# A two-layer decoder step on one core: layer 1's sparse attention reordered around its index scores, the third expert's gate and up weights loaded during the router, a split first chunk and split final stores

## The reference, cut to what matters

```python
def _dsa_attention(q, k, v, qi, ki, wi, q_pos):
    n_sel = min(TOPK_MAX, nk // 4)                 # 64 of 256 keys (prompt), 256 of 1032 (sample)
    def one(blk):
        dots = jnp.einsum('bqhd,bkd->bqhk', bqi, ki)             # 8 index heads of 64
        score = jnp.einsum('bqh,bqhk->bqk', bwi * idx_scale, jax.nn.relu(dots))
        score = jnp.where(mask[None], score, -jnp.inf)
        _, idx = lax.top_k(score, n_sel)
        ...                                         # gather the selected keys and values
        s = jnp.einsum('bqhgd,bqkhd->bqhgk', bq, ks) * (HD_B ** -0.5)   # 16 heads on 4 key heads of 64
        p = jax.nn.softmax(jnp.where(valid, s, -jnp.inf), axis=-1)
        o = jnp.einsum('bqhgk,bqkhd->bqhgd', p, vs)

x = _layer_norm(ALPHA * x + h, ...)
x = _layer_norm(ALPHA * x + _moe(x, ...), ...)      # one of 4 groups, 2 experts in it; d_ff 512
x = x + sigmoid(x @ ple_gate_w[i] + ple_gate_b[i]) * (p[i] @ ple_proj[i])
```

## Time and profile before

| what | value |
| --- | --- |
| median of 3 runs | 1469.85 us (1469.12 to 1471.43) |
| profiled execution, its own time | 1466.78 us |
| its span | 1465.0 us |
| mean granted TensorE clock | 0.923 of full speed |
| PE busy | 1221.9 us, 83% of the span |
| DVE busy | 490.7 us, 33% |
| ACT busy | 343.6 us, 23% |
| POOL busy | 42.0 us, 3% |
| HBM read and written | 341.48 and 21.97 MB, 248 GB/s over the span |

### The profile page before, as it was taken

The page is one execution under the profiler, slowest core; times in us unless marked ns, Lnnn a source line. Parts: engine busy times, 40 slices in busy tenths (PEclk is TensorE's granted clock), DMA queues, the critical chain, the costliest instruction groups (busy, mean ns, idle before and its releaser), DMA issues.

```text
span 1465.0 us, 19098 instructions
## 1 busy us (share of the span) xinstructions
PE 1221.9 (83%) x6655; PEld 615.5 (42%) x6656; DVE 490.7 (33%) x1067; ACT 343.6 (23%) x807; POOL 42.0 (3%) x70
## 2 busy tenths in 40 slices
PE   6998888869589999995999831799884999999855
PEld 3445666645333333332444501556542333333322
DVE  1012555532611111116211679544242111111163
ACT  1113444441111112111111410455310212121110
POOL 1100000001000000001000100000100000000100
PEclk8999999999699999997999965999986999999978
DMA  9935799967248999995511433153440979999721
GB/s 336 414 135 209 266 351 373 344 265 317 87 189 349 363 425 426 423 421 172 211 37 30 137 120 110 44 187 116 151 152 12 390 287 408 424 426 424 299 85 36
DMA packets 97599, 364.50 MB, mean 249 GB/s; under 512 B 17856, under 2 KB 34272, under 8 KB 75760
## 3 DMA queue, kind: packets, MB, share of 16 engines
q1 hardware_dynamic: 88512, 328.79, 58.0%
q0 software_dynamic: 6320, 25.78, 5.1%
q10 hardware_dynamic: 2688, 8.91, 1.6%
HBM read 341.48 MB, written 21.97 MB: 248 GB/s over the span
## 4 chain that ended last, share of the span: by engine, by line
PE 72%; DVE 13%; DMA 6%; issue 4%; ACT 4%; POOL 0%; DVEq 0%; SPq 0%; POOLq 0%; ACTq 0%
PE PS L574 17%; PE PS L856 14%; PE PS L877 7%; PE PS L829 6%; PE PS L985 5%; DMA ring<-in_moe_w_up 3%; PE PS L707 2%; PE PS L670 2%; PE PS L657 2%; DVE PR L2043 2%; DVE PR L2041 2%; PE PS L838 2%; PE PS L608 1%; PE PS L1174 1%; PE PS L866 1%
## 5 line engine op out<-in xcount | busy, mean ns | idle before, releaser
L574 PE MATMUL PS<-ring,XT 128*128 128x512 f32 (+3 forms) x960 | 255.2, 478 | 12.5 <-DMA ring<-in_a_w_in 7.0
L856 PE MATMUL PS<-ring,QKV 128*64 128x512 f32 (+1 forms) x512 | 228.7, 595 | 6.8 <-ACT QKV L1206 3.9
L859 PE MATMUL PS<-ring,QKV 128*64 128x512 f32 (+1 forms) x512 | 228.5, 595 | 0.0
L1206 ACT ACTIVATE QKV<-PS 128x512 f32<-128x512 f32 (+5 forms) x180 | 95.0, 528 | 393.2 <-PE PS L574 156.6
L574 PEld LDWEIGHTS PS<-ring,XT 128*128 128x128 f32 (+1 forms) x960 | 121.0, 165 | 144.7 <-issue 127.2
L856 PEld LDWEIGHTS PS<-ring,QKV 128*64 128x64 f32 (+1 forms) x512 | 71.2, 141 | 151.5 <-issue 145.6
L877 PE MATMUL PS<-ring,QKV 128*64 128x512 f32 (+1 forms) x512 | 123.8, 598 | 0.0
L829 PE MATMUL PS<-X,QKV 128*64 128x512 f32 x432 | 103.3, 614 | 19.2 <-issue 19.2
L1850 DVE TENSOR_TENSOR QKV<-QKV,PS 64x512 f32<-64x512 f32 (+1 forms) x32 | 21.7, 680 | 234.3 <-ACT QKV L1390 234.3
L1855 DVE COPY QKV<-PS 64x512 f32<-64x512 f32 (+1 forms) x32 | 22.2, 693 | 189.1 <-PE PS L877 189.1
L985 PE MATMUL PS<-ring,XT 128*128 128x512 f32 (+1 forms) x256 | 74.8, 507 | 7.7 <-ACT XT L1206 7.7
(11 more groups left out here) (284 smaller groups left out, 1305.5 us busy)
## 6 DMA issues: line engine op xcount, KB each, us to landing
ring<-in_moe_w_gate SPq DMA_DIRECT2D x32, 2048.0 KB, 11.1
ring<-in_moe_w_up SPq DMA_DIRECT2D x32, 2048.0 KB, 15.8
ring<-in_moe_w_down SPq DMA_DIRECT2D x32, 2048.0 KB, 13.4
ring<-in_cache_a_k SPq DMA_DIRECT2D x64, 512.0 KB, 5.8
ring<-in_cache_a_v SPq DMA_DIRECT2D x64, 512.0 KB, 5.6
ring<-in_a_w_in SPq DMA_DIRECT2D x6, 2048.0 KB, 20.2
places<-OR POOLq DMA_DIRECT2D x8, 1024.0 KB, 19.1
ring<-in_ple_gate_w SPq DMA_DIRECT2D x4, 2048.0 KB, 13.4
```

Source lines behind the costliest of these rows:

```text
L574: ins = pe.matmul(PS[p0:p1, banks[u % 4], 0:c1 - c0], XT[:, k, t0:t0 + rows], wt[:, k, c0:c1], start=(k == 0), stop=(k == KD - 1))
L856: ins = pe.matmul(PS[0:m, 0, :], XE[:, k, 0:m], wg[:, k, :], start=(k == 0), stop=(k == KD - 1))
L859: ins = pe.matmul(PS[p1:p1 + m, 1, :], XE[:, k, 0:m], wu[:, k, :], start=(k == 0), stop=(k == KD - 1))
L1206: ins = act.activation(dst, src, ACT.Copy) if scale is None else \
```

## The change

The diff has 1365 lines. Its parts are:

1. **Start.** The first chunk of `a_w_in` comes as two loads of 1 MB with a semaphore each (`first_columns_landed` for the first), and PE waits for the second one only at its fifth matmul. POOL's load of the 955.5 KB of constants moves behind its small loads and waits for the first half chunk. Only the upper 64 rows of each expert's `places` are zeroed, by 16 DMAs in place of 8.
2. **Third expert.** The buffers QB, OR, KP, PR and SM become one tensor (WIDE), and expert 2's gate and up weights are loaded into it: the gate when the logits are there, the up weights when the norm is done. The first two pairs of experts are written out ahead of PE's loop, which starts at pair 2. SP then loads expert 4's gate and up as soon as expert 0's are used. POOL loads the second norm's parameters, which lie in the same buffer, after expert 2 has used its up weights.
3. **Layer 1.** The columns of `b_w_in` are loaded in another order, the index columns first, as two chunks of 292; the kidx pages come right after them, then the other three chunks, then all keys, then all values. PE turns the tokens and projects the index columns only (tiles 0, 2, 1), turns the kidx pages, computes prompt index scores (by 64-row halves of the operands, with no zeroes) and sample scores; only then come the nine other units, while DVE selects for the prompt and sorts for the sample. A half of the sort has 520 columns. q and k are rotated after the sort. All keys and queries are turned ahead of the batches, the keys in place in the ring. The selection runs on 128 partitions at once. In the batches, prompt scores use 64-row halves, the values of request b-1 are multiplied within batch b, and the prompt's values come out transposed, so that no turn of outputs follows.
4. **End.** Six stores, each as soon as its half of a tile is ready.

```diff
+B_COLUMNS = ((1536, 1828), (1828, 2120), (0, 512), (512, 1024), (1024, 1536))
+INDEX_UNITS = ((0, 0, 7), (1, 0, 5), (0, 2, 6), (1, 2, 4), (0, 1, 7), (1, 1, 5))
...
-            for j in range(5):
-                s.add(("b_in", j), ("qkv_mm1", 3 * j + 3))
-            s.add("kidx", ("kidx_mm", 8), DB * NPAGE)
+            for j in range(2):
+                s.add(("b_in", j), ("qkv_mm1", 5 + j))
+            s.add("kidx", ("sis_mm", 9), DB * NPAGE)
+            for j in range(2, 5):
+                s.add(("b_in", j), ("qkv_mm1", 3 * j + 3))
             for pr in range(4):
-                s.add(("kb", pr), ("kbt_mm", 8 * pr + 8), 2 * NPAGE)
+                s.add(("kb", pr), ("sb_mm", 2 * pr + 2), 2 * NPAGE)
+            for pr in range(4):
                 s.add(("vb", pr), ("pvb_mm", 2 * pr + 2), 2 * NPAGE)
...
-        HALF = 512 + NS
+        HALF = 512 + DQ
...
+            w0 = a_w_in[0].rearrange("(p k) n -> p k n", k=KD)
+            s0 = place(("a_in", 0))
+            for half, sem in ((0, S("first_columns_landed")), (1, landed[s0])):
+                sp.dma_start(ring[:, s0, 2048 * half:2048 * half + 2048].rearrange("p (k n) -> p k n", k=4),
+                             w0[:, 4 * half:4 * half + 4, 0:512]).then_inc(sem, 16)
...
+                sp.wait_ge(*at(f"logit_mm{layer}", 1))
+                load(2, 0, EARLY[0], S(f"early_gate{layer}"))
+                sp.wait_ge(*at(f"normed{layer}0", 3))
+                load(2, 1, EARLY[1], S(f"early_up{layer}"))
+                for j in range(2):
+                    used(0, j)
+                    chunk(2, j)
+                for j in range(2, 6):
+                    used(0, j)
+                    chunk(1, j)
+                for j in range(2, 6):
+                    used(1, j)
+                    chunk(2, j)
+                with sp.Fori(3, NE // 2) as i:
...
+            pool.wait_ge(S("first_columns_landed"), 16)
+            a, n = CONST["ident"]
+            pool.dma_start(C[:, a + n:], consts[:, a + n:]).then_inc(S("setup_landed"), 16)
...
                 pool.wait_ge(*at(f"normed{layer}0", 3))
+                pool.wait_ge(*at(f"experts_used{layer}", 3 * 2 + EXPERT_USED[1]))
                 norm_params(1)
...
+            for j in range(2):
+                for t, (t0, n) in enumerate(TILES):
+                    pool.wait_ge(*at("gated1", 3 * j + t + 1))
+                    pool.dma_start(token_rows(y_p[0], y_s.rearrange("b q d -> (b q) d"), t)[:, 512 * j:512 * j + 512],
+                                   X[0:n, t, 512 * j:512 * j + 512]).then_inc(S("stored"), 16)
...
+            n_kidx, s_kidx = item("kidx")
+            pe.wait_ge(landed[s_kidx], stream.landed[n_kidx])
...
+            kidx_sum(3)
+            for u in range(6, 15):
+                if u >= 8:
+                    pe.wait_ge(*at("qkv_evac1", u - 1))
+                unit(u // 3, u % 3, (6, 4)[u % 2])
...
+            for g in range(4):
+                keys_turn(g)
+            pe.wait_ge(*at("sorted", SEL_SAMPLE // 8))
...
+            queries_turn(0)
+            queries_turn(1)
+            for g in range(6, 16):
+                keys_turn(g)
...
             for b in range(DB):
-                batch_b(b)
+                if b >= 1:
+                    pe.wait_ge(*at("bat_evac", 3 * b))
+                sample_scores(b, 1)
+                if b == 0:
+                    pe.wait_ge(*at("kbt_evac", 18))
+                prompt_scores(b)
+                sample_scores(b, 0)
+                new_scores_b(b)
+                if b >= 1:
+                    values_b(b - 1)
+                prompt_turn(b)
+                weights_turn_b(b)
+                prompt_values(b)
+            values_b(DB - 1)
```

More of the change, by code:

```diff
@@ L415, in _, with chunk, used @@
+                def chunk(i, j):
+                    s = (n0 + j) % SLOTS
+                    load(i * 2 + j // 3, j % 3, ring[:, s, :], landed[s])
+                def used(i, j):
+                    sp.wait_ge(*at(f"experts_used{layer}", i * 6 + (3 * (j // 3) + EXPERT_USED[j % 3])))
                 for j in range(6):
                     n = n0 + j - SLOTS
-                    before = layer == 0 and n < 6
-                    expert(j // 3, j, (lambda j=j: sp.wait_ge(*at("pv_mm", DB - 1 if j < 2 else DB))) if before else
-                           (lambda n=n: sp.wait_ge(*at(stream.used[n][0], stream.used[n][1]))))
@@ L420, in _ @@
-                with sp.Fori(1, NE // 2) as i:
+                    if layer == 0 and n < 6:
+                        sp.wait_ge(*at("pv_mm", DB - 1 if j < 2 else DB))
+                    else:
+                        sp.wait_ge(*at(stream.used[n][0], stream.used[n][1]))
+                    chunk(0, j)
+                sp.wait_ge(*at(f"logit_mm{layer}", 1))
+                load(2, 0, EARLY[0], S(f"early_gate{layer}"))
+                sp.wait_ge(*at(f"normed{layer}0", 3))
+                load(2, 1, EARLY[1], S(f"early_up{layer}"))
@@ L943, in down, with pair @@
                         pe.sem_inc(S(f"experts_used{layer}"), 1)
[L945 to L946 removed]
+                def pair(i):
                     for u in range(7):
@@ L951, in experts_dense @@
                             down(i, u - 1)
+                pe.sem_inc(S(f"experts_used{layer}"), 1)
+                pair(0)
+                pair(1)
+                with pe.Fori(2, NE // 2) as i:
+                    pair(i)
             def gated_input(layer):
@@ L1090, in _, with kidx_scores @@
-            kidx_sum(7)
-            pe.wait_ge(*at("kidx_evac", 8))
+            def kidx_scores(r):
+                pe.wait_ge(*at("kidx_evac", min(r + 3, 4)))
+                for half in range(2):
+                    if r >= 2:
+                        pe.wait_ge(*at("si_relu", 2 * (r - 2) + half + 2))
+                    pe.matmul(PS[:, 2 * (r % 2) + half, :], QIB[:, r, :], kidx[:, r, 512 * half:512 * half + 512],
+                              start=True, stop=True).then_inc(S("sis_mm"), 1)
@@ new lines, in kidx_sum @@
+            def kidx_sum(r):
+                pe.wait_ge(*at("si_relu", 2 * r + 3))
+                for half in range(2):
+                    ins = pe.matmul(PS[NS * half:NS * half + NS, 5, :], WS[:, r, :],
+                                    RELU[r % 2][:, 512 * half:512 * half + 512], start=(r == 0), stop=(r == 3))
+                ins.then_inc(S("si_sum_mm"), 1)
+            new_scores()
+            kidx_scores(0)
+            new_sum()
+            for r in range(1, 4):
+                kidx_scores(r)
+                kidx_sum(r - 1)
```

765 lines of the change are left out of this document (424 added, 341 removed).

## The result

The changed kernel takes **1373.77 us** (median) where the kernel before took 1470.23 in the same comparison: ratio 0.9345, 95% interval 0.9328 to 0.9361. The forecast was 1391 with a range of 1368 to 1418: right in sign and inside the range, but the gain was 96 us and the forecast had 79. The time lies just under the 1378 to 1404 that the forecast gave by itself, and inside the range through the bounds that the range took in.

A forecast was written before the change was run, and what follows sets the result against it. The prediction took PE as the bound, idle while DVE sorts in layer 1. From the profiled 1466.78 us it took 70.7 (attention), 5.1 (start) and 2.8 (end): 1388.2, or 1391 on the median; range 1368 to 1418.

The forecast's parts named there:

- The main term: Layer 1's attention: projection beside the sample sort, sort ending 62.7 us earlier; with later stages -70.7 us, bounds -45 to -86.
- Its cover must be real: Layer 1's sort: PE's units and key turns end at 843 and 848, the sort at 845.2, with nothing to spare.
- PE waits some 6 us there: Layer 1, before turning index keys: PE ready at about 758, last kidx page landed at 763.5.
- But its chain is longer than that ... I get 12.3: Layer 1's batch loop: a serial chain over several engines sets 12.3 us a batch, 98.4 us for eight.
- the lower bound taken from PE's work (10.8): Layer 1's batch loop: 10.8 us a batch if PE's remaining work alone decides.
- the loop keeps 15.0 us: Rival, layer 1's batches: the DVE and ACT chain decides, so the pace stays; 1413 us, chance 0.22.
- row halves run together: Rival, layer 1's scores: two 64-row halves run side by side, up to 6 us more gained; 1385 us, chance 0.10.
- The early weights: Third expert's weights loaded early: forecast 0, bounds -3.4 to +5; rival that they end last experts' waits, 1388 us, chance 0.05.
- the projection does not hide: Rival, layer 1: columns loaded behind 64 pages come after the index scores; 51 us return, 1442 us, chance 0.03.
- SP's pace: Slower rival, layer 1's kidx pages: slow SP issues hold PE; 2.4 us a page eats the gain, 2.6 gives 1484; chance 0.04.
- The start: First projection chunk: half-chunk load and constants moved behind it let PE start earlier; -5.1 us, bounds -2.5 to -8.4.
- The end: Final stores: only 128 KB left when the last sixth is ready; -2.8 us, bounds -1 to -3.2.

## Why the prediction was right, and where it was off

**The main term held.** A round of the sort went from 1.63 to 1.53 us (1.52 predicted), the 32 rounds took 49.0 us (48.5), and the projection lay beside it with nothing to spare: the units ended at 846.81, the sort at 847.48 (843 and 845.2 on the marks of before). "Its cover must be real" was right, and the run with the units after the sort puts 55 us on it. Of the rest of the attention's gain, the row halves' 5.1 us in the batches is tested; no run turns the keys inside the batches again, so what that move is worth is read from the marks alone (34.4 us less in batches and tail, 9.7 more ahead of them). All in all the attention gained 86.4 us, at the very end of the bounds of 45 to 86.

**The pages.** "PE waits some 6 us there": it was 9.15. SP was held twice, 3.94 us at the second load of columns and 3.19 at the first page, where the sum had one start without a hold; the bound of 5.75 later held it. From the landing to the sort it took 30.1 us where the sum had 33.2, nearly all of the difference ahead of the prompt's first round (16.0 us, the sum had 19). So the sort began within 2 us of the mark that the sum had for it (798.45, 796.7), because a wait too short and a stretch too long cancelled. The 1.4 us charged for the clock behind that wait were about right: without the wait the same stretch ran at 1.00 and took 1.7 us less.

**The term that failed is the batch.** "But its chain is longer than that ... I get 12.3" was 16.3 us too much over eight batches (82.1 measured, 98.4 predicted). That is more than the whole error of the forecast's spans, 14.4. The chain in order of time through one batch of the changed kernel (its longest pieces):

```profile
893.59 1.08 PE PS L1265 x4
894.67 0.86 PE PS L1267 x4
895.53 0.88 PE PS L1285 x8
896.43 0.44 DVE XT L2270
896.89 0.42 DVE small L2273
897.31 0.61 DVE XT L2270
897.95 0.69 DVE small L2273
898.63 1.21 DVE small L2276
900.13 0.29 DVE XT L2283
900.99 0.36 DVE XT L2284
901.39 0.66 PE PS L1297 x4
902.05 0.98 PE PS L1319 x9
903.04 0.81 PE PS L1307 x12
903.86 1.08 PE PS L1265 x4
```

There is indeed a chain, with 5 us of DVE in it (896.4 to 901.4), and doubling the row maximum shows that it decides. But it has no exponential: the request's runs on ACT beside DVE's scaling of the prompt's weights and PE's turn of them, and half the request's scores come behind the prompt's, beside the masks. I had put the prompt's and the request's steps one behind the other; they run side by side, and PE fills the 5 us with the values of the request before (2.3 us) and the rest of the scores. The prediction gives no sizes for most of its steps, so how its 2 us too many divide among them can't be told; the request's exponential, which it counts and the chain lacks, takes 1.17 us. So PE is busy 9.89 of 10.26 us while a chain through two engines closes the round: the lower bound taken from PE's work (10.8) was the better figure, 0.54 too high, and the row halves, 0.64 a batch, account for that. The terms given for that bound come to another figure, though: 13.91 less 3.9 is 10.0.

**Rivals.** That the loop keeps 15.0 us is refuted by 10.26. That row halves run together was given 0.10 and priced at 6 us; it is true, with 5.1 us in the batches. So the forecast's "I count no gain" for them was wrong as well. The early weights gave nothing, as forecast and for the reason given (slots full while expert 3 runs); they could not be seen in the total at the 15th expert either, but their waits went. That the projection does not hide: refuted. SP's pace: the mechanism is there, at 0.52 us an issue; the pages came 1.1 us apart as before.

**Small terms.** The start gave 4.3 of 5.1, its two parts nearly as priced. The end gave 2.7 to 3.3 of 2.8. The prediction's reading that stores 0.57 us apart land together was wrong: the three of before landed 3.1 to 4.6 us after their issues, at 1456.5, 1458.1 and 1459.1. The three more stores cost nothing for another reason: five of the six go out before the last half is ready, and the last one landed 2.2 us after its issue, not 2.9. Two slips of the sums change nothing: 22.3 less 9 is 13.3 and not 12.9, and 63 times 1.28 is 81 and not 79. What the sum had not: layer 0 spent the start's gain, 5.6 us in all. Its last batch's value matmuls took 5.89 us for 72 records instead of 4.23, part of them at the lower clock level; its first expert took 16.2 us instead of 14.5; and four experts instead of two waited for weights, some 1.6 us more. These three make 5.0 of the 5.6. Undoing the early loads left the first expert at 16.2, so they are not its cause; the other runs' experts waited two to four times. In layer 1, 2.1 us were gained between the output projection and the experts, and the fourth expert took 25.2 us instead of 26.9; no experiment took these apart.

## What to carry to other kernels

When one engine has a long stretch alone, ask which independent work could lie beside it, and make the sum of both lists in one order; here that one move was worth 55 of 93 us. For a pipelined loop, lay out the chain once around, with two things that run side by side counted once, before adding up instructions: a serial sum was 2 us a batch too long. A lead in a stream of loads is only worth something if it is still there where the waits are; and a share of the chain is not its worth until it is known what comes next behind it.

## What was not expected of the hardware

- With a wait of 1.26 us in each batch of some 12 us, parts of the loop ran at the lower of the two clock levels: 0.92 granted over the batches, where the changed kernel, idle 0.37 us a batch, had 0.99. So the instruction of 1.28 us cost 2.06 us a batch.
- The first expert behind the router takes 14.5 or 16.2 us. In the slower case the first ten records run in pairs up to 0.85 us apart, at a granted clock of 0.50, then 0.43 apart at 1.00. In layer 0 it was 16.2 in every kernel with the new order and 14.5 before, in layer 1 it was either. What decides it stays open.
- Two 64-row halves of fp32 matmuls ran 1.7 times as fast as the same records on one half (0.93 and 1.57 us for eight records).
- 4.4 MB of weights issued 33 to 39 us earlier, ahead of a store of 256 KB, delayed it (it landed 6.3 us after its issue instead of 3.1) and, behind it, the gathers by 3 to 4 us; 20 page loads of 32 KB in the same place did not.
